# Walking the columns of the dense three-pass matmuls from the last to the first

## The reference, cut to what matters

```python
p = _split_in(hN @ w_in[l])                      # 1024 -> all projections of block 1
merged = (jax.nn.sigmoid(p["g_a"]) * (ya @ w_branch_a[l])
          + jax.nn.sigmoid(p["g_b"]) * (yb @ w_branch_b[l]))
x = x + merged @ w_out[l]
...
gate, up = jnp.split(h @ w_in, 2, axis=-1)       # feed-forward, twice
return (jax.nn.silu(gate) * up) @ w_out
...
proj = h @ mix_w_in                              # projections of the mixer
```

## Time and profile before

| what | value |
|---|---|
| median of 3 runs | 1961.77 us (1957.5 to 1962.15) |
| the profiled execution's own time | 1959.44 us |
| its span in the trace | 1957.7 us |
| granted TensorE clock, mean | 0.995 of full speed |
| PE busy | 1920.9 us, 98% of the span |
| PEld busy | 1586.1 us, 81% |
| DVE, ACT, POOL busy | 51%, 38%, 10% |

### The profile page before, as it was taken

One profiled execution on the slowest core, in us unless ns is written; L12 is line 12 of the kernel. 1 busy time (PEld: TensorE's weight loads), 2 busy tenths in 40 slices (PEclk: granted clock), 3 DMA queues, 4 the chain that ended last, 5 costly groups with the idle time before them and its releaser, 6 DMA issues.

```text
span 1957.7 us, 25809 instructions
## 1 busy us (share of the span) xinstructions
PE 1920.9 (98%) x9544; PEld 1586.1 (81%) x9544; DVE 1008.2 (51%) x1413; ACT 738.5 (38%) x1293; POOL 192.5 (10%) x242
## 2 busy tenths in 40 slices
PE   7999999999999999999999999999999999999998
PEld 5888878766688888888887788899888888888887
DVE  6787866575454563333334666445643573333332
ACT  4344333465532342222222664333523352222332
POOL 1101110000000000000011235035000000000010
PEclk9999999999999999999999999999999999999999
DMA  8967912311043323333333333210334323333331
GB/s 317 323 171 243 307 46 89 86 33 44 22 117 115 102 87 96 96 96 94 108 89 100 85 87 87 73 47 15 105 97 134 107 87 107 96 96 94 95 100 56
DMA packets 330903, 212.89 MB, mean 109 GB/s; under 512 B 21373, under 2 KB 315450, under 8 KB 330302
## 3 DMA queue, kind: packets, MB, share of 16 engines
q1 hardware_dynamic: 319830, 170.27, 30.0%
q0 software_dynamic: 10368, 37.75, 5.5%
q10 hardware_dynamic: 616, 3.67, 0.5%
HBM read 204.31 MB, written 7.35 MB: 108 GB/s over the span
## 4 chain that ended last, share of the span: by engine, by line
PE 92%; DVE 4%; DMA 2%; ACT 1%; issue 1%; SPq 1%; POOL 0%; DVEq 0%; POOLq 0%; ACTq 0%
PE psum L435 26%; PE psum L437 25%; PE psum L436 25%; PE psum L1471 2%; PE psum L1257 1%; PE psum L1289 1%; PE psum L989 1%; PE psum L990 1%; PE psum L991 1%; PE psum L1270 1%; DMA ada_w<-in_ada_w 1%; DVE delta_qkv_T L2223 1%; DVE ada_sum L2223 1%; PE psum L1155 1%; PE psum L1171 1%
## 5 line engine op out<-in xcount | busy, mean ns | idle before, releaser
L435 PE MATMUL psum<-act_hi,w_hi 128*128 128x512 f32 x1616 | 648.4, 401 | 4.8 <-DVE act_lo L2223 2.5
L437 PE MATMUL psum<-act_hi,w_lo 128*128 128x512 f32 x1616 | 631.2, 391 | 0.0
L436 PE MATMUL psum<-act_lo,w_hi 128*128 128x512 f32 x1616 | 630.5, 390 | 0.0
L394 DVE TENSOR_TENSOR w_lo<-w_raw,w_hi 128x1024 fp32r<-128x1024 f32 x306 | 382.2, 1252 | 316.3 <-ACT w_hi L386 294.3
L386 ACT ACTIVATE w_hi<-w_raw 128x1024 fp32r<-128x1024 f32 x306 | 319.4, 1051 | 181.8 <-PE psum L437 174.3
L435 PEld LDWEIGHTS psum<-act_hi,w_hi 128*128 128x128 f32 x1616 | 304.0, 188 | 83.2 <-issue 19.6
L437 PEld LDWEIGHTS psum<-act_hi,w_lo 128*128 128x128 f32 x1616 | 303.8, 188 | 65.2
L436 PEld LDWEIGHTS psum<-act_lo,w_hi 128*128 128x128 f32 x1616 | 304.3, 188 | 60.8 <-issue 1.4
L765 POOL TENSOR_TENSOR squares<-squares 128x512 f32<-128x512 f32 x18 | 28.9, 1605 | 1238.4 <-ACT squares L1659 1238.4
L435 PE MATMUL psum<-ffn_hi,w_hi 128*128 128x512 f32 (+1 forms) x374 | 141.7, 379 | 0.0
L437 PE MATMUL psum<-ffn_hi,w_lo 128*128 128x512 f32 (+1 forms) x374 | 140.9, 377 | 0.0
(11 more groups left out here) (369 smaller groups left out, 2344.0 us busy)
## 6 DMA issues: line engine op xcount, KB each, us to landing
w_raw<-in_ffn_w_in SPq DMA_DIRECT2D x88, 512.0 KB, 3.7
ada_w<-in_ada_w POOLq DMA_DIRECT2D x72, 512.0 KB, 5.4
w_raw<-in_w_in SPq DMA_DIRECT2D x68, 512.0 KB, 3.8
w_raw<-in_mix_w_in SPq DMA_DIRECT2D x52, 512.0 KB, 3.7
w_raw<-in_ffn_w_out SPq DMA_DIRECT2D x32, 512.0 KB, 4.1
w_raw<-in_ffn_w_out SPq DMA_DIRECT2D x16, 384.0 KB, 3.3
w_raw<-in_w_branch_a SPq DMA_DIRECT2D x8, 512.0 KB, 4.0
w_raw<-in_w_out SPq DMA_DIRECT2D x8, 512.0 KB, 3.9
```

The lines of the kernel that those rows point to most:

```text
L394: dve.tensor_tensor(WLO[:, n % 4, :], RAW[:, n % 4, :], WHI[:, n % 4, :].bitcast(F32), ALU.subtract).then_inc(w_lo, 1)
L435: pe.matmul(out, whi, hhi, start=start, stop=False)
L436: pe.matmul(out, whi, hlo, start=False, stop=False)
L437: return pe.matmul(out, wlo, hhi, start=False, stop=stop)
```

## The change

One line is added to `mm3`. It replaces the output and the two moving operands by views of the same columns with a step of -1: the last column is read and written first. The stationary operands are not touched. Column n of the activation still goes to column n of the bank. The number, the order, the sizes and the semaphores of the instructions on all engines are the same as before; only the line numbers behind L434 are one higher.

```diff
@@ -432,6 +432,7 @@
 
         def mm3(pe, out, whi, wlo, hhi, hlo, start, stop):
 
+            out, hhi, hlo = out[:, ::-1], hhi[:, ::-1], hlo[:, ::-1]
             pe.matmul(out, whi, hhi, start=start, stop=False)
             pe.matmul(out, whi, hlo, start=False, stop=False)
             return pe.matmul(out, wlo, hhi, start=False, stop=stop)
```

## The result

The changed kernel takes 1997.01 us (median of 4 runs, 1996.2 to 1997.86) against 1960.47 us for the kernel before (4 runs, 1957.5 to 1962.15). The ratio is 1.0186, with a 95% interval of 1.0171 to 1.0201: **1.9% slower, some 37 us**. The forecast was no change.

The account below looks back on a forecast made before the run. PE was taken as the bound, through mm3's three passes. With 0 ns per matmul for the reversal and 0 for every other engine, the time stayed at 1961 us; the range was 1955 to 3425 us.

Parts of the forecast that it names:

- The bound and the lever: PE's mm3 matmuls bound the kernel; 1 ns more or less per matmul is 6.9 us, 0.35% of the time.
- I take 0: Reversed read and write in mm3 cost 0 ns per matmul, taken with little confidence from the nearest trace rows.
- the ends: Bounds for the reversed mm3 access: 0 ns, or 203 to 213 ns per wide matmul at the plain float32 rate.
- L1570's four separate runs: Pooling product, 512 moving columns in four runs: as fast as L1189's single run, so no restart cost was seen.
- The other support of the 0: mm3's moving read: four descending columns still hit each 16-byte SBUF line, so by the skill's two-hit rule it costs nothing.
- Rival B: Moving read or PSUM write in mm3: half rate if descending neighbours aren't paired, 203 to 213 ns per matmul; chance 0.35.
- Rival C: Start of each reversed mm3 row: fixed price at any width, doubling 13.4 ns gives 93 us, middle 1985 us; chance 0.09.
- The weight load "is covered, with 39 ns to spare": The weight load beside each wide mm3 matmul takes 188 ns of its 226.7 ns, so it is hidden.
- the 13.4 ns: Fixed part of each mm3 matmul beyond its columns' cycles, same at 256 and 512 columns, assigned to the instruction's start.
- The prediction's last sentence: In mm3, the forecast would fail in a small way if the fixed 13.4 ns hung on where a row begins.
- Every other engine's term is 0: Outside TensorE: same instructions, waits, semaphores and bytes, so no reader starts earlier or later; 0 us.
- The write side: mm3's PSUM output written backwards: taken to cost 0 ns per matmul.

Follow-up runs that it names:

- second kernel of streams: Matmuls alone, 52 per section, the middle 40 timed, with the order of moving columns and the width varied; fp32r at 512 columns: 226.7 ns forward, 233.5 backward.
- e1: The changed kernel with only the moving operands of mm3 reversed, output forward: 1995.09 us against 1956.61 for the kernel before, ratio 1.0195.
- e3: The changed kernel with mm3's columns reversed only inside each group of four, groups ascending: 1957.42 us against 1958.5 for the kernel before, ratio 0.9996.
- e4: The changed kernel with mm3's groups of four columns descending, each walked forward inside: 1996.86 us, ratio 1.0199 to the kernel before.
- the streams: Five kernels of matmuls alone, varying access pattern, width, weights and placement, each run once; plain forward fp32r sections at 512 columns agree within 226.5 to 227.2 ns.
- e5: The kernel before, all forward, with 64 bytes left free ahead of w_hi, shifting weights and everything behind: 1983.83 us against 1956.12, ratio 1.0132.
- e6: The changed kernel with 64 bytes left free ahead of w_hi, shifting weights and everything behind: 1997.16 us, ratio 1.0201 to the kernel before.

## Why the prediction was right or wrong

**The bound and the lever: right.** The wide matmul's distance from start to start times its count set the time; 1 ns per matmul was said to be 6.9 us, and 6.7 ns at the 6798 wide ones make 45 us, of which 37 were seen.

**"I take 0": wrong.** The step that failed is the choice between the ends for the read of the moving row. The rows it leaned on could not show it. L1570's four separate runs were runs of 128 columns, and whole runs of 128 are free even in descending order (226.7 ns in the second kernel of streams); they were also plain float32, which pays for no direction. The prediction called the rows weak for both of these reasons and took their value all the same. What a row of the right kind would have had to be, full-rate fp32r with another order inside 256 bytes, the trace of before didn't contain. In place of 0 the read of the moving row costs 6.7 ns at 512 columns (e1). The other support of the 0, that four neighbours share 16 bytes in either direction, was true inside a group (e3, 226.7 ns) and said nothing of the order of the groups, which is what costs (e4, 233.3). Nor are two hits on 16 bytes enough for full speed in this stream: at a step of 2, 256 columns took 226.4 ns in place of 119.7.

**Rival B: wrong, by its own deciding point.** The steps of 2, which take about twice the time on both sides, fit pairs, but two neighbours in descending order are handled in one step. It held 0.35, and the upper end of the range with it.

**Rival C: the right size, the wrong mechanism.** Its span, 0.8 to 13.4 ns a matmul, held the 6.7 ns, and its 1985 us lies near 1997. But it put the price at the far end of the row, fixed for every width, and the half-wide matmuls would have had to pay the same amount. They went from 120.0 to 118.5 ns. It also was given 0.09, which was too little: a price of a few cycles per instruction needs no failure of the hardware, only a small stall, and the lever of 6.9 us per ns made any such stall visible.

**The weight load "is covered, with 39 ns to spare": the deeper mistake.** That the load runs beside the matmul and ends in time was right, and was taken to mean that it costs nothing. Yet by the place of the weights against the moving row alone the forward matmul moves between 226.5 and 236.7 ns. I had found the 13.4 ns that 512 columns take beyond their cycles, and had set them aside as belonging to "the start of an instruction" because they were the same at 256 columns. They aren't constant: by the forward sections of the second kernel of streams what is left beyond the columns' cycles is 13.4 ns at 512 columns, 16.8 at 504, 13.3 at 384 and 11.7 at 288. That they might be a meeting of two reads, which a reordering would change, was not among the rivals. The prediction's last sentence did say that they might hang on where a row begins, and gave this neither a price nor a chance. The Trainium skill, "TensorE: Matmul & The Clock Gate", in the step on LDWEIGHTS of Part 2, says that the two reads have independent ports and that loading the next weights doesn't steal bandwidth from the running matmul. The runs differ, and they decide: in fp32r the forward stream takes between 226.5 and 236.7 ns by nothing but the places of the two operands.

**Every other engine's term is 0: right** to what the traces show; the busy times of DVE, ACT and POOL are those of before. **The write side: right**, 1.0003.

**What is shown and what is not.** Shown: the price is on the read of the moving row, in fp32r, and it comes from the order of the 16-byte groups within runs shorter than 64 columns (e1 to e4, the streams). Shown as well: with nothing turned round, moving the weights by 64 bytes against the moving row costs the same 6.7 ns, in streams and in the large kernel (e5), and in steps of 64 bytes the two places count modulo 256 bytes. That the backward price and the placement price have one cause is argued, not shown. For it: the same size, the same 256 bytes (descending runs of 64 columns are free), no sum of the two in e6. Against a simple form of it: the descent costs 6.3 ns on top of a row with skipped groups. Not shown: that the weight load is the partner, by a stream without one; which part of the memory the two reads would share; why the stall has these sizes, and why the width moves it as it does.

## What to carry to other kernels

When one instruction shape fills the chain, work out its distance from start to start, compare it with its columns times the cycle, and treat any rest as something that the operands' order and place may change, not as a constant. For fp32r streams keep the moving rows ascending, lay moving rows and weight tiles out at the same place modulo 256 bytes, and begin both at a multiple of 8 columns (both from 4 or from 2 cost 230.0 and 233.2 ns). 64 bytes put in between cost this kernel 1.3% with no instruction changed. Turning the output round was free, and so was the descending order of whole runs of 64 or 128 columns that are each walked forward.

## What the runs showed of the hardware that was not expected

- An fp32r matmul of 512 columns takes 226.5 to 236.7 ns in a dense forward stream, depending only on where the moving row and the 128 stationary columns lie; 218.8 ns when one group of four columns is read again and again; bf16 takes 215.7 to 216.0 in either direction.
- A smaller weight load can make the stream slower: at 512 moving columns 226.5 ns with 128 stationary columns, 230.0 with 64, 231.5 with 32. At 256 moving columns it makes it faster: 113.2 ns with 64 in place of 120.0 with 128.
- Writing to PSUM with a step of 2 takes twice the time (214.7 against 110.0 ns for 256 columns of bf16), writing with a step of -1 the same time.
- At 256 columns and a full weight load the backward read is 1.1 to 1.8 ns faster than the forward one; with 64 stationary columns it is 4.8 ns slower.
